# RWKV scan of a two-block layer stack on one core: step 11's mask before the update, squares and clamp behind the last context tap, blend in two instructions, centering and V's third tap one place later

## The chip, the cores and the metric

The kernel runs on one core of one Trainium2 chip. The metric is the time of one execution in device microseconds (us), given as the median of several runs. A second number, the span, is what one profiled execution took from its first to its last instruction. TensorE (PE) multiplies, VectorE (DVE), ScalarE (ACT) and GpSimd (POOL) do the elementwise work, SyncE (SP) issues the DMAs.

## The reference

A first block is an RWKV-7 mixer with a context, a spatial gating branch and an expert-choice feed-forward network; a second block has differential attention, a recurrent unit and neighbourhood attention. The change touches the RWKV part (`token_mixer`, `context_scan_states`) and one wait of the stage behind it. All is fp32. What matters, cut down:

```python
z = centred_shift(h @ w_in, taps)     # z[t] = y[t-1]*w0 + y[t]*w1 + y[t+1]*w2: three taps
r, k, v, dwf, dwb, daf, dab, dg = split(z)
d = exp(-exp(-softplus(-(w0 + tanh(dw) @ w2)) - 0.5))       # one for each direction
a = sigmoid(a0 + da @ a2)
kk = k * k_k;  kk = kk * rsqrt(maximum(sum(kk*kk), 1e-12))  # square, squares, clamp, root, invert
k_dir = k * (1 + (a - 1) * k_a)                             # blend: 1 + (a-1)*k_a, then times k
# scan forward and backward, over 256 context tokens and then 512 tokens:
S = S*d - (S kk)(kk*a)^T + v k^T ;  y = S r
y = ((y - mean) * rsqrt(var + eps)) * lnx_g + lnx_b         # center, variance, normed
y = (y + (sum(r*k*r_k)) * v) * (sigmoid(dg) @ g2)           # bonus, gated
```

The stage behind it (`stage_merge`) makes the gating branch and the outputs, and beside that the modulation vectors (`silu(c) @ ada_w`), in 20 column blocks of 512, on VectorE.

## The kernel before, in words

`stage_scan` treats the 16 heads in 8 pairs, 128 channels each. One pair is one turn j of the loops (turns 0 to 8; the ninth only finishes the last pair). The tokens, context and main, make 12 steps of 64; both directions are computed together. In place of a token-by-token scan, the system of a step is inverted in five levels, four steps at a time (a group).

Each turn has three stretches s (groups of four steps of this pair), each with five levels l, and each level two halves: places (s, l, 0) and (s, l, 1). Every engine walks through the same loops and has a function `beside(j, at)` that puts other work at each place: for the next pair (b = j + 1) projections, taps, decay, rates and the parts of kk and k; for the previous pair (a = j - 1) centering, variance, bonus and gate. So the order of the queues is written out by hand; only semaphores tie the engines together. In turn j the scan's own steps 8 to 11 of pair j - 1 run in stretch 0, steps 0 to 7 of pair j in stretches 1 and 2.

What TensorE does at a level: the product X times the part (L752), with tokens turned in between (`product_beside_tokens`, L737) and keys (L909); right side and scores (L854, L721); `beside` of the first half; solve (L894); correct (L832, L834); read-out (L921); `beside` of the second half. At level 4 there is no solve; there `correct_last` (L814, L817) waits for two things: the level's mask from VectorE, and `xt0_done`, GpSimd's word that the next group's start matrix is ready. The chain to that is: `parts` on VectorE (L1626, masks the scores of a step), `part_moved` on ScalarE (L1265, copies four steps), `xt0` on GpSimd (L1466 and L1468, two passes over 128x512).

VectorE at a level: `mask` (L1539), `beside`, `update` (L1550, L1552), `state` (L1565, L1569), `beside`. ScalarE: `negate` (L1207), `beside`, `solved` (L1212, which TensorE's read-out waits for), `beside`. GpSimd's queue in a turn: `xt0(j, 1)`, `reverse_v(j + 1, 0)` (L1509, waits for V's context taps), `xt0(j, 2)`, `new_k(j + 1)` (L1476 to L1478, wait for blend), `scaled_k`, `xt0(j + 1, 0)`, and so on.

Short results of TensorE go through `Scratch`: three banks of PSUM, handed out in turn in the order in which TensorE's program takes them. Whoever takes one waits until the last user of that bank has moved its contents:

```python
def take(self, pe, *what):
    n, R = len(self.nth), len(self.banks)      # R = 3
    self.nth[what] = n
    if n >= R:
        pe.wait_ge(self.moved[n % R], n // R)
```

Names at the places of the change: `squares` (L684) sums k's squares per head on TensorE from `square` (L1276); `clamp` (L1639), `root` (L1281), `invert` (L1644), `widen` (L1286), then transposes back to TensorE (L695) and `unit_k` (L1651). `shift` applies taps (L1607, L1609, L1611: first, second, third). `blend` is L1294, `gated` L1719. `center` (L950) writes the centered y, which ScalarE copies twice (L1328, L1329). TensorE's projection of the next pair's K (L673, at (0, 0, 1)) waits until all taps of V are done. SyncE's queue (weights of the next pair) isn't changed.

In `stage_merge` TensorE makes a list of outputs; ahead of output 32 (the first "mix") stand value, u and gate outputs, then come mix 0, mix 1, a 0, mix 2, a 1. `conds_turned` says behind which output a column block of the modulation is summed over channels (L198). VectorE adds the bias (L206) once all 20 are turned, and only then empties the mix outputs' banks (L2171, L2172).

Of the kernel before, what the change touches and what calls it, by code (L numbers as in the profile page):

```python
# [502 lines left out]
def stage_scan(k, hT, w_low, low_loaded, th, da, sg, ya, spare, m, first_chunk, first_loaded, loose, h_scale):  # L503
# [20 lines left out]
    with ExitStack() as s:  # L524
# [91 lines left out]
        def _(pe):  # L616
# [28 lines left out]
            def context_of(j, d):  # L645

                if live(j):
                    from_low_rank(j, (("rate", d, 1), ("decay", 1 - d, 1)))
# [297 lines left out]
            def center(j):  # L946
                if live(j):
                    pe.wait_ge(S["y_copied"], j + 1)
                    o = sc.take(pe, "center", j)
                    sc.fill(mm(o[:], m["center"][:], yj[:], start=True, stop=True), "center", j)  # L950
# [29 lines left out]
            def beside(j, at):  # L980

                a, b = j - 1, j + 1
                if at == (0, 0, 0):
                    turn_params(b)
                if at == (0, 0, 1):
                    project(b, K_X, 0)
                if at == (0, 1, 0):
                    project(b, K_X, 1)
                    bonus(j)
                if at == (0, 1, 1):  # L990
                    project(b, K_X, 2)
                if at == (0, 2, 1):
                    project(b, K_X, 3)
                if at == (0, 2, 0):
                    both_directions(b, "rate")
                if at == (0, 3, 0):
                    both_directions(b, "decay")
                if at == (0, 3, 1):
                    to_tokens(j, "B", 0)
                if at == (0, 4, 0):  # L1000
                    context_of(b, 0)
                    to_tokens(j, "K", 0)
                if at == (0, 4, 1):
                    context_of(b, 1)
                    center(a)
                    project(b, K_V, 0)
                if at == (1, 0, 0):
                    variance(a)
                if at == (1, 0, 1):
                    project(b, K_V, 1)  # L1010
                if at == (1, 1, 0):
                    project(b, K_V, 2)
                    spread_rstd(a)
                if at == (1, 1, 1):
                    project(b, K_V, 3)
                if at == (1, 2, 1):
                    gate(a)
                if at == (1, 3, 1):
                    project(b, R_X, 0, KT)
                    project(b, R_X, 1, KT)  # L1020
                    squares(b)
                if at == (1, 4, 0):
                    project(b, R_X, 2, KT)
                if at == (1, 4, 1):
                    project(b, R_X, 3, KT)
                if at == (2, 0, 0):
                    spread_inverse(b)
                if at == (2, 0, 1):
                    project(b, R_X, 4, KT)
                if at == (2, 1, 0):  # L1030
                    project(b, R_X, 5, KT)
                if at == (2, 1, 1):
                    project(b, R_X, 6, KT)
                if at == (2, 2, 0):
                    project(b, R_X, 7, KT)
                if at == (2, 2, 1):
                    scores(b, 0)
                    scores(b, 2)
                if at == (2, 3, 1):
                    for i in range(3):  # L1040
                        project(b, V_X, i, KT)
                if at == (2, 4, 0):
                    for i in range(3, 5):
                        project(b, V_X, i, KT)
                if at == (2, 4, 1):
                    for i in range(5, KT):
                        project(b, V_X, i, KT)
# [152 lines left out]
        def _(act):  # L1200
            f = act.activation
# [84 lines left out]
                    f(sqj.rearrange("p (n c) -> p n c", c=HEAD), length[:].rearrange("p t h -> p (t h)").unsqueeze(2).to_broadcast([P, 2 * NT, HEAD]),  # L1286
                      ACT.Copy).then_inc(S["inverse_wide"], 1)

            def blend(j):

                if live(j):
                    for i in range(4):
                        sc.settled(act, "rate", j, i)
                    f(kt[:], ra[:], ACT.Identity, scale=col(j, 10), bias=col(j, 18)).then_inc(S["t1_done"], 1)  # L1294

            of_seg = (slice(0, CTX_STEPS), slice(CTX_STEPS, STEPS))
            each_way = lambda view: view.rearrange("p d (n t) -> p d n t", t=HEAD)
# [42 lines left out]
            def beside(j, at):  # L1340
                a, b = j - 1, j + 1
                if at == (0, 0, 0):
                    tokens(j, "V", 0)
                if at == (0, 2, 1):
                    rate(b, 0)
                    rate(b, 1)
                if at == (0, 3, 0):
                    decay(b, 0)
                if at == (0, 3, 1):
                    part_moved(j, 1)  # L1350
                    decay(b, 1)
                    tokens(j, "B", 0)
                if at == (0, 4, 0):
                    rate(b, 2)
                    decay(b, 3)
                    tokens(j, "K", 0)
                    copy_y(a)
                if at == (0, 4, 1):
                    x0(j, 1)
                    rate(b, 3)  # L1360
                    decay(b, 2)
                    centered(a)
                if at == (1, 0, 0):
                    tokens(j, "V", 1)
                    deviation(a)
                if at == (1, 0, 1):
                    widen_rstd(a)
                if at == (1, 1, 0):
                    tokens(j, "B", 1)
                if at == (1, 2, 0):  # L1370
                    tokens(j, "K", 1)
                if at == (1, 3, 0):
                    tokens(j, "V", 2)
                if at == (1, 3, 1):
                    square(b)
                    part_moved(j, 2)
                    root(b)
                if at == (1, 4, 0):
                    tokens(j, "B", 2)
                if at == (1, 4, 1):  # L1380
                    x0(j, 2)
                    widen(b)
                    if j == KT - 1:
                        act.wait_ge(S["ahead_mm"], 1)
                        sc.settled(act, "inverse", KT - 1, 0)
                        sc.settled(act, "inverse", KT - 1, 1)
                        t, o = AHEAD[0]
                        f(spare[:, t, 0:512], bank[o][:], ACT.Copy).then_inc(S["ahead_moved"], 1)
                if at == (2, 0, 0):
                    tokens(j, "K", 2)  # L1390
                    blend(b)
                if at == (2, 0, 1):
                    grow(b, 0)
                    shrink(b, 0)
                if at == (2, 1, 0):
                    grow(b, 1)
                if at == (2, 1, 1):
                    shrink(b, 1)
                if at == (2, 2, 0):
                    shrink_r(b)  # L1400
                if at == (2, 2, 1):
                    decay_over_step(b)
                if at == (2, 3, 1):
                    part_moved(b, 0)
                if at == (2, 4, 1):
                    x0(b, 0)
# [7 lines left out]
            def prologue():  # L1414
# [15 lines left out]
                decay_over_step(0)  # L1430
                for i in range(4):
                    rate(0, i)
                blend(0)
                part_moved(0, 0)
                x0(0, 0)
                act.wait_ge(S["low_shift"], low_no(LOW_GATE))
# [94 lines left out]
        def _(dve):  # L1531
# [188 lines left out]

            def beside(j, at):
                a, b = j - 1, j + 1
                if at[0] < 2 and at[1] < 4 and at[2] == (1 if at[0:2] == (1, 3) else 0):
                    parts(j, 4 + 4 * at[0] + at[1])
                if at == (0, 0, 0):
                    params(b)
                if at == (0, 1, 1):
                    bonus(j)
# [13 lines left out]
                    shift(b, K_V, (0,))  # L1742
                if at == (1, 2, 1):
                    shift(b, K_V, (1,))
                if at == (1, 3, 0):
                    shift(b, K_V, (2,))
                    gated(a)
                if at == (1, 3, 1):
                    clamp(b)
                if at == (1, 4, 0):  # L1750
                    invert(b)
                if at == (1, 4, 1):
                    running_sums(b, 1)
                if at == (2, 0, 1):
                    unit_k(b)
# [14 lines left out]
                    scaled_b(b, 1)  # L1770
                    scaled_q(b, 1)
                if at == (2, 4, 1):
                    shift(b, V_X)

            def low_shift(f):

# [51 lines left out]
def stage_merge(k, hT, ya, x1, retired, first_chunk, first_loaded, ring1, u, ys, gates, xn, aff, ring, w_in_ex, loose, lt, iota_i, iota):  # L1828
# [14 lines left out]
    for i in range(8):  # L1843
# [17 lines left out]
    CONDS_LOADED_BEHIND = {1: range(0, 2), 2: range(2, 4), 3: range(4, 6), 4: range(6, 9), 5: range(9, 12),  # L1861
                           6: range(12, 15), 7: range(15, 18), 8: range(18, len(ADA))}
    CONDS_TURNED_BY = {1: range(0, 3), 2: range(3, 6), 3: range(6, 9), 4: range(9, 12), 5: range(12, 14), 6: range(14, 17),
                       7: range(17, len(ADA))}
    conds_turned = {4 * c + 1 + len(AHEAD): CONDS_TURNED_BY[c] for c in CONDS_TURNED_BY}
    names = """x_in sgu_in ln1_in w_turned w_moved made moved_act moved_dve v_normed stats std iota_made iota_done lt_made row_mm row_moved
        diag_made l_stats l_std r_stats r_std sc2_made rows_mm rows_moved router_in normed turned turn_moved logits shifted e_done""".split()
    S = {n: k.sem("mg_" + n) for n in names}
# [1828 lines left out]
```

## Time and profile before

| what | us |
|---|---|
| median of 3 runs | 2960.75 (2954.12 to 2962.56) |
| the profiled execution, its own time | 2963.89 |
| its span | 2962.3 |
| PE busy | 2726.9 (92%) |
| DVE busy | 1170.3 (40%) |
| ACT busy | 608.7 (21%) |
| POOL busy | 265.6 (9%) |
| mean granted TensorE clock | 0.979 |

Busy times are sums over all instructions of an engine. The scan lies between some 100 and 880 us of the span; turn 3, from which most rows below are, begins at 402 and ends at 499, turn 7 begins at 793. In the profile's rows a line such as L1626 is the line of the kernel, and `arena`, `x` and `bank` are names of shared buffers. A matmul of fp32 is two records. Consecutive rows of one engine overlap a little, since instructions are pipelined.

### The profile page before, as it was taken

The numbers are of one execution on the slowest core, as the hardware profiler recorded it, in microseconds if no ns is written. First come the engines' busy times: TensorE is split into PE (matmuls) and PEld (weight loads), VectorE is DVE, ScalarE is ACT, GpSimd is POOL, SyncE is SP. The second block draws the span as 40 slices with busy tenths as digits, with TensorE's granted clock in tenths as the row PEclk, the third lists the DMA queues.
The fourth block names the chain that finished last, engine by engine and source line by source line (L and its number), as shares of the span: only waits on it lengthen the run. The fifth ranks groups of instructions, "written<-read, shape, count | busy, mean of one in ns | idle before, by whom it ended". The sixth has DMA issues, their size and how long they took to land. (4 is left out here: it accounts for less than half of the span.)

```text
span 2962.3 us, 69542 instructions
## 1 busy us (share of the span) xinstructions
PE 2726.9 (92%) x31106; PEld 1478.0 (50%) x31106; DVE 1170.3 (40%) x2615; ACT 608.7 (21%) x1254; POOL 265.6 (9%) x282
## 2 busy tenths in 40 slices
PE   6999999999989999979988988989886999999998
PEld 3667676777664445444343333433333555455553
DVE  4566556656634762271211221212013255423333
ACT  2324333333221100010000000000002344323322
POOL 1221122212200000010000000000000111110000
PEclk9999999999999999989999999999998999999999
DMA  5000000000007872349999999999994421042210
GB/s 206 27 25 21 21 20 26 21 21 18 33 5 267 301 256 85 133 195 377 431 430 431 430 430 431 431 430 430 431 430 170 144 59 37 0 134 64 63 34 29
DMA packets 188812, 557.41 MB, mean 188 GB/s; under 512 B 29452, under 2 KB 117026, under 8 KB 163958
## 3 DMA queue, kind: packets, MB, share of 16 engines
q1 hardware_dynamic: 188534, 553.19, 47.6%
q8 instruction: 237, 3.88, 0.5%
q14 instruction: 41, 0.34, 0.0%
HBM read 550.65 MB, written 2.24 MB: 187 GB/s over the span
## 5 line engine op out<-in xcount | busy, mean ns | idle before, releaser
L2338 PE MATMUL bank<-arena,xe 128*64 128x512 f32 x1024 | 351.9, 614 | 36.1 <-DMA gates<-in_exp_w_dram 19.9
L2338 PEld LDWEIGHTS bank<-arena,xe 128*64 128x64 f32 x1024 | 108.6, 141 | 189.5 <-issue 177.4
L673 PE MATMUL bank<-arena 128*128 128x512 f32 x384 | 191.9, 620 | 1.2 <-issue 1.2
L3361 PE MATMUL bank<-arena 128*128 128x512 f32 x384 | 173.8, 600 | 1.9 <-PEq L2656 1.9
L2338 PE MATMUL bank<-arena,hidT 128*64 128x512 f32 x512 | 170.0, 595 | 2.5 <-DMA gates<-in_exp_w_dram 2.0
L2789 PE MATMUL bank<-arena 128*128 128x512 f32 x320 | 145.2, 602 | 1.2 <-ACT arena L2937 1.2
L2551 DVE TENSOR_TENSOR x<-x,bank 128x512 f32<-128x512 f32 x64 | 43.7, 686 | 232.9 <-PE bank L2376 232.9
L2338 PE MATMUL bank<-mg_ring,xe 128*64 128x512 f32 x256 | 114.5, 601 | 20.0 <-DMA u<-in_exp_w_dram 20.0
L2338 PE MATMUL bank<-ys,xe 128*64 128x512 f32 x256 | 115.9, 606 | 16.5 <-DMA arena<-in_exp_w_dram 15.8
L2544 DVE TENSOR_TENSOR hid<-hid,bank 128x512 f32<-128x512 f32 x32 | 19.8, 682 | 280.3 <-PE bank L2338 280.3
L1539 DVE TENSOR_TENSOR pm<-bank,m_level 128x512 f32<-128x512 f32 x120 | 82.8, 690 | 102.3 <-PE bank L752 101.6
L2338 PE MATMUL bank<-gates,xe 128*64 128x512 f32 x256 | 118.2, 616 | 0.0
L2338 PE MATMUL bank<-u,xe 128*64 128x512 f32 x256 | 114.9, 602 | 0.0
L834 PE MATMUL bank<-XT,pm 64*64 64x32 f32 x3072 | 111.2, 220 | 2.2 <-issue 1.9
L832 PE MATMUL bank<-pm,XT 64*64 64x32 f32 x3072 | 107.0, 218 | 3.9 <-issue 2.2
L3361 PEld LDWEIGHTS bank<-arena 128*128 128x128 f32 x384 | 69.9, 190 | 81.1 <-issue 81.1
L752 PEld LDWEIGHTS bank<-X,px 64*64 64x64 f32 x2560 | 85.7, 135 | 44.6 <-issue 19.1
L832 PEld LDWEIGHTS bank<-pm,XT 64*64 64x64 f32 x3072 | 99.4, 135 | 6.7 <-issue 3.2
L752 PE MATMUL bank<-X,px 64*64 64x64 f32 x2560 | 98.4, 224 | 3.0 <-issue 1.5
L834 PEld LDWEIGHTS bank<-XT,pm 64*64 64x64 f32 x3072 | 99.4, 134 | 3.4 <-issue 3.3
L2789 PEld LDWEIGHTS bank<-arena 128*128 128x128 f32 x320 | 59.7, 193 | 74.0 <-issue 73.4
L1207 ACT ACTIVATE x<-bank 128x128 f32<-128x128 f32 x96 | 26.7, 278 | 331.7 <-PE bank L854 331.7
(523 smaller groups left out, 5542.1 us busy)
## 6 DMA issues: line engine op xcount, KB each, us to landing
arena<-in_exp_w_dram SPq DMA_DIRECT2D x96, 2048.0 KB, 26.7
gates<-in_exp_w_dram SPq DMA_DIRECT2D x24, 2048.0 KB, 29.9
ys<-in_exp_w_dram SPq DMA_DIRECT2D x24, 2048.0 KB, 26.7
mg_ring<-in_exp_w_dram SPq DMA_DIRECT2D x24, 2048.0 KB, 26.8
u<-in_exp_w_dram SPq DMA_DIRECT2D x24, 2048.0 KB, 31.3
ws_w<-in_ada_w_dram SPq DMA_DIRECT2D x40, 1024.0 KB, 5.6
arena<-in_odd_w_in_dram SPq DMA_DIRECT2D x32, 512.0 KB, 3.9
arena<-in_w_in_dram SPq DMA_DIRECT2D x24, 512.0 KB, 3.9
```

The lines of the kernel that those rows point to most:

```text
L673: last = mm(to[:], wj[:, c, i, :], hT[:, c, 0:T], start=(c == 0), stop=(c == KT - 1))
L752: last = mm(INV[c, cs(q)], part(4 * g + q // 2, q % 2, 0, 0)[h], X[h, (j * GROUPS + g) % 2, q, :], start=True, stop=True)
L832: mm(into(INV, h, q), XT[c, g, q, :], blocks(pm[c, q, :], b, 0), start=True, stop=True)
L834: last = mm(into(INVT, c, q), pm[c, q, :], blocks(XT[c, g, q, :], b, 1), start=True, stop=True)
L1207: f(rn, RIGHT.rearrange("p (d v) -> p d v", d=2), ACT.Copy, scale=-1.0).then_inc(S["r_neg"], 1)
L1539: tt(pm[:], INV[:].rearrange("p (q t) -> p q t", q=8), m["level"][:, l, :].unsqueeze(1).to_broadcast([P, 8, HEAD]), ALU.mult).then_inc(S[" ...
L2338: r[e] = mm(out[a, :], lhs[j][:, a], w[:, j, 512 * c:512 * c + 512], start=(first and j == 0), stop=(last and j == len(lhs) - 1), skip_gro ...
L2544: dve.tensor_tensor(hid[:, f, :], hid[:, f, :], bank[4 + f][:], ALU.mult).then_inc(S["hid_made"], 1)
L2551: dve.tensor_tensor(x1[:, n, c], x1[:, n, c], bank[scatter_bank(q, o)][:], ALU.add).then_inc(S["added"], 1)
L2789: last = mm(o[:], w[:, c, i, :], hT[:, i, :], start=(i == 0), stop=(i == KT - 1))
L3361: last = mm(o[:], w[:, i, t, :], hT[:, t, :], start=(t == 0), stop=(t == KT - 1))
```

## The change

At (1, 3) VectorE's `parts` of step 11 runs in the first half, behind the mask and ahead of the update, and the third tap of K's and V's context and `gated` go to the second half. ScalarE copies the part before it squares. `squares` on TensorE, `clamp` on VectorE and `root` on ScalarE go from (1, 3, 1) to (1, 4, 0), `invert` from (1, 4, 0) to (1, 4, 1). `blend` becomes two instructions, one per direction, at (2, 0, 0) and (2, 0, 1). `center` stands behind the first projection piece of K's and V's context at (0, 4, 1). V's third tap goes from the end of a turn, (2, 4, 1), to (0, 0, 0) of the next, behind `parts`. In `stage_merge` column block 19 is turned behind output 34 instead of 32.

```diff
@@ TensorE, beside
                 if at == (0, 4, 1):
                     context_of(b, 1)
+                    project(b, K_V, 0)
                     center(a)
-                    project(b, K_V, 0)
@@
                 if at == (1, 3, 1):
                     project(b, R_X, 0, KT)
                     project(b, R_X, 1, KT)
+                if at == (1, 4, 0):
                     squares(b)
-                if at == (1, 4, 0):
                     project(b, R_X, 2, KT)
@@ ScalarE
-            def blend(j):
+            def blend(j, way):
 
                 if live(j):
-                    for i in range(4):
-                        sc.settled(act, "rate", j, i)
-                    f(kt[:], ra[:], ACT.Identity, scale=col(j, 10), bias=col(j, 18)).then_inc(S["t1_done"], 1)
+                    if way == 0:
+                        for i in range(4):
+                            sc.settled(act, "rate", j, i)
+                    last = f(kt[:, way], ra[:, way], ACT.Identity, scale=col(j, 10), bias=col(j, 18))
+                    if way == 1:
+                        last.then_inc(S["t1_done"], 1)
@@
                 if at == (1, 3, 1):
+                    part_moved(j, 2)
                     square(b)
-                    part_moved(j, 2)
-                    root(b)
                 if at == (1, 4, 0):
                     tokens(j, "B", 2)
+                    root(b)
@@
                 if at == (2, 0, 0):
                     tokens(j, "K", 2)
-                    blend(b)
+                    blend(b, 0)
                 if at == (2, 0, 1):
+                    blend(b, 1)
                     grow(b, 0)
                     shrink(b, 0)
@@ VectorE, beside
-                if at[0] < 2 and at[1] < 4 and at[2] == (1 if at[0:2] == (1, 3) else 0):
+                if at[0] < 2 and at[1] < 4 and at[2] == 0:
                     parts(j, 4 + 4 * at[0] + at[1])
                 if at == (0, 0, 0):
+                    if j:
+                        shift(j, V_X, (2,))
                     params(b)
@@
-                if at == (1, 3, 0):
+                if at == (1, 3, 1):
                     shift(b, K_V, (2,))
                     gated(a)
-                if at == (1, 3, 1):
+                if at == (1, 4, 0):
                     clamp(b)
-                if at == (1, 4, 0):
+                if at == (1, 4, 1):
                     invert(b)
-                if at == (1, 4, 1):
                     running_sums(b, 1)
@@
                 if at == (2, 4, 1):
-                    shift(b, V_X)
+                    shift(b, V_X, (0, 1))
@@ stage_merge
-                       7: range(17, len(ADA))}
+                       7: range(17, 19)}
     conds_turned = {4 * c + 1 + len(AHEAD): CONDS_TURNED_BY[c] for c in CONDS_TURNED_BY}
+    conds_turned[34] = range(19, len(ADA))
```

## Rows read from the trace of the kernel before

**Rows 1.** The page, part 1: busy us of each engine (share of the span).

```profile
PE 2726.9 (92%) x31106; PEld 1478.0 (50%) x31106; DVE 1170.3 (40%) x2615; ACT 608.7 (21%) x1254; POOL 265.6 (9%) x282
```

**Rows 2.** Waits of PE, 165 to 860 us: engine line <- released by: total us, times, longest.

```profile
PE bank L814 <- issue: 15.0, 12, 3.0
...
PE bank L921 <- ACT x L1212: 3.5, 8, 0.5
...
PE bank L950 <- ACT X L1271: 2.1, 6, 0.4
```

**Rows 3.** Timeline of DVE, turn 3, (1, 3): start, us, engine, line [idle before <- releaser].

```profile
454.03 0.69 DVE L1539 TENSOR_TENSOR pm<-bank,m_level 128x512 f32<-128x512 f32 x1 [0.22 <-PE bank L752]
454.64 0.47 DVE L1611 SCALAR_TENSOR_TENSOR kj<-bank,pcol,kj 128x255 f32<-128x255 f32 x1
...
455.54 0.75 DVE L1719 SCALAR_TENSOR_TENSOR arena<-arena,pcol,bank 128x512 f32<-128x512 f32 x1
...
457.99 0.29 DVE L1569 TENSOR_TENSOR ZG<-Z,g 128x128 f32<-128x128 f32 x1
458.20 0.68 DVE L1626 TENSOR_TENSOR px<-bank,m_part 128x512 f32<-128x512 f32 x1
```

**Rows 4.** Timeline of ACT, turn 3, (1, 3) to (1, 4).

```profile
459.07 1.27 ACT L1265 ACTIVATE XT<-px 64x512 f32<-64x512 f32 x2 [2.41 <-DVE px L1626]
...
464.84 0.83 ACT L1286 ACTIVATE x<-k_length 128x768 f32<-128x768 f32 x1
```

**Rows 5.** Timeline of POOL, turn 3, (1, 3) to (1, 4).

```profile
455.57 0.40 POOL L1509 COPY vjr<-vj 128x256 f32<-128x256 f32 x1 [27.33 <-DVE vj L1611]
460.42 1.27 POOL L1466 TENSOR_TENSOR XT<-XT,m_pair 128x512 f32<-128x512 f32 x1 [4.45 <-ACT XT L1265]
461.77 1.26 POOL L1468 TENSOR_TENSOR XT<-XT,m_id 128x512 f32<-128x512 f32 x1
```

**Rows 6.** Timeline of PE, turn 3, (1, 3) to (1, 4).

```profile
458.86 0.58 PE L684 MATMUL bank<-head_ones,x 128*32 128x2 f32 x48
459.37 0.27 PE L752 MATMUL bank<-X,px 64*64 64x64 f32 x2
...
460.47 1.12 PE L673 MATMUL bank<-arena 128*128 128x512 f32 x2
463.13 0.25 PE L814 MATMUL bank<-XT,pm 64*64 64x32 f32 x2 [1.54 <-issue]
```

**Rows 7.** Timeline of PE, turn 7: L814 of (1, 4), read-out of (2, 0).

```profile
849.84 0.32 PE L814 MATMUL bank<-XT,pm 64*64 64x32 f32 x2 [2.98 <-issue]
...
857.89 0.42 PE L921 MATMUL bank<-x 64*64 64x64 f32 x7
```

**Rows 8.** Windows: stretch, length, busy us (instructions) of the engines, PEclk, DMA, GB/s.

```profile
849.84:856.08 6.24, 5.54 (x153) 5.01 (x154) 1.11 (x2) 1.69 (x4) 0.00 (x0) 0.50 0.03 5
...
463.13:470.13 7.00, 6.19 (x232) 4.88 (x232) 3.21 (x5) 3.85 (x7) 0.14 (x1) 1.00 0.02 5
...
1115.50:1118.90 3.40, 3.40 (x8) 1.73 (x7) 3.33 (x11) 0.00 (x0) 0.00 (x0) 0.50 0.77 293
```

**Rows 9.** Timeline of ACT, turn 3, (2, 0).

```profile
468.25 1.67 ACT L1294 ACTIVATE kt<-ra,pcol 128x1536 f32<-128x1536 f32 x1
469.81 0.27 ACT L1212 ACTIVATE x<-bank 128x128 f32<-128x128 f32 x1
```

**Rows 10.** Timeline of PE, turn 3, (2, 0).

```profile
470.13 0.45 PE L921 MATMUL bank<-x 64*64 64x64 f32 x8 [0.49 <-ACT x L1212]
```

**Rows 11.** Timeline of DVE, turn 3, (2, 0).

```profile
471.14 0.81 DVE L1569 TENSOR_TENSOR ZG<-Z,g 128x128 f32<-128x128 f32 x1
```

**Rows 12.** Timeline of DVE, end of turn 3.

```profile
498.32 0.75 DVE L1611 SCALAR_TENSOR_TENSOR vj<-bank,pcol,vj 128x511 f32<-128x511 f32 x1
```

**Rows 13.** Timeline of PE in the merge stage.

```profile
1114.35 0.43 PE L198 MATMUL bank<-ones,arena 128*32 128x1 f32 x32 [1.92 <-DVE arena L186]
```

**Rows 14.** Timeline of DVE in the merge stage.

```profile
1117.46 0.69 DVE L2172 TENSOR_TENSOR ys<-ys,u 128x512 f32<-128x512 f32 x1
```

More of the change, by code:

```diff
@@ L1432, in prologue @@
                     rate(0, i)
-                blend(0)
+                blend(0, 0)
+                blend(0, 1)
                 part_moved(0, 0)
```

## The prediction

> **What bounds the kernel now.** I read the page's busy shares first, then the waits of TensorE over seven turns of the scan, then the timelines of single places. TensorE is busy 92% of the span [rows 1], so a moved step counts only where TensorE now waits for it. Its list of waits [rows 2] gives three places that the change touches: L814, the correction at place (1,4), 15.0 us in 12 waits; L921, the read-out at (2,0), 3.5 us in 8, released by ScalarE; and L950, the centering at (0,4), 2.1 us in 6, released by a ScalarE copy. The list names "issue" for L814 and so hides the cause; the timelines show it.
>
> In turn 3 VectorE ends ZG (L1569) at 458.28 and the mask of step 11 (L1626) runs only then, from 458.20 [rows 3]; ScalarE copies the part from 459.07 for 1.27 us [rows 4]; GpSimd makes two passes, 460.42 to 463.03 [rows 5]; TensorE, whose two projection matmuls began at 460.47 and took 1.12, starts L814 at 463.13, 0.1 us behind GpSimd, after 1.54 us of idleness [rows 6]. That is a chain mask, copy, two passes, correction, and it starts too late.
>
> **Part 1, step 11's mask and its company.** The mask now follows the level's mask, which ends at 454.72 [rows 3]. It comes 3 us earlier, and the whole chain with it. The stall doesn't vanish by its 1.5 us, because two things move the other way.
>
> First, `squares` moves behind the product of (1,4), so the turned tokens B of group 2 are now taken one place before it, and take over the scratch bank that `squares` had: the one held by `gate` of the turn before. TensorE must wait there for `gated`, and `gated` has moved behind update and state. Queued ahead of it on VectorE are both context taps (454.64 to 455.54, 0.90 us as a pair) and then itself (0.75). It starts where L1626 did: 458.20 + 0.90 + 0.75 = 459.85, and 0.1 us for the release: 459.95. TensorE could have begun the product at 458.86, where `squares` began [rows 6]. So 1.1 us of new waiting, with the whole product, key update, right side and correction queued behind it.
> Then the sum for turn 3: 459.95, product 1.10 (459.37 to 460.47), squares 0.51 (458.86 to 459.37), projection 1.07 = 462.63, against 463.13: 0.5 us gained.
>
> Second, GpSimd reverses V's context between the two passes of group 1 and of group 2, and it waits for the last context tap. That tap now ends at 459.07; 0.06 release, 0.40 reversal, 0.04, 2.61 for the passes, 0.1: L814 not before 462.3 [rows 3, 5]. That is hidden under 462.63 by 0.3 us and is what is late next if the bank's wait were shorter. Square, clamp, root and invert move with the tap: `square` runs 459.1 to 460.1, before TensorE wants it at 461.1; the level's mask waits for the product and ends at 461.9; clamp and root end before the correction does at 463.6, and `invert` (0.22 us) stands ahead of a scan (1.8 us) with 0.8 us free behind it. Cost nothing; without that cover `widen` (0.83 [rows 4]) would slip by the 0.2 of `invert`.
>
> The same sum over each turn's own times gives 0.8 in turn 0 (no gate there, GpSimd decides), 0 in turn 1 (the copy is earlier there), 0.2 in turn 2, 0.5 in turns 3 to 6, and in turn 7 (no tap, no squares) L814 from 849.84 to 847.9, 1.9 us. Sum 4.9. Bounds: 0, if a new wait eats it all, and 13.6, the idleness at these eight places (15.0 less what stands elsewhere).
>
> **The clock in turn 7.** There TensorE idles 2.98 us before L814 [rows 7], and the granted clock is 0.50, the lower level of 1.2 GHz, in the 6.24 us behind it [rows 8]. From L814 to the read-out of (2,0) the turn takes 8.05 us [rows 7]; turn 3 takes 7.00 (463.13 to 470.13), some 1.1 of it the blend's stall and the inverse's transposes, which turn 7 lacks. So the low level costs 2.2 us. The new wait there is 1.1 us, shorter than the 1.54 of turn 3 [rows 6], behind which the clock stayed at 1.00 [rows 8]. I take 2.2; the ends are 0 and 3.1, half of 6.24.
>
> **Part 2, blend in halves.** ScalarE spends 1.67 us on blend and copies U (L1212) only at 469.81 [rows 9]; the read-out starts at 470.13 after 0.49 us [rows 10]. A half costs about 0.86: the 768-element row takes 0.83 [rows 4]. U is then copied at 469.0, and the read-out follows the correction at 469.5: 0.6 us in turns 2 to 6, 0.2 in turn 0, none in turn 1, where TensorE is later anyway; sum 3.2. The second half then precedes the table load, which starts at 470.1 as before; the next negation is wanted at 472.6, and ScalarE is free at 472.6. GpSimd starts on K 0.1 us later and is needed at 479. Ends: 0 and 3.9, 0.65 in six turns.
> ZG (L1569) took 0.81 us here, not its 0.29, beside GpSimd's pass over K [rows 11, 3]. It will be asked for 0.6 us sooner but ends when that pass does, at 471.95; unit_k and the next level's mask then end at 473.7, and TensorE wants that mask at 473.7. So no loss, but no room either; if it slips, up to 0.1 us a turn is given back.
> The Trainium skill, SBUF — State Buffer, "Who interferes with whom", says that VectorE and GpSimd share a port pair that one instruction holds to its end, also for a VectorE operation with two SBUF inputs. ZG is such an operation and the trace agrees (0.81 against 0.29). By this rule it blocks for what is left of GpSimd's pass, as reckoned; if it did not, ZG would be early and the sum would be the same.
>
> **Part 3, centering behind the projection.** L950 waits for the copy of X (L1271), which frees its bank, 0.35 us on average [rows 2]; matmuls back to back overlap by 0.07, so 0.43 is filled by the projection's 2.0 us. Six turns: 2.6. The centered copies on ScalarE come 1.5 us later, still 0.3 before the next negation. Ends 0 and 2.8.
>
> **Part 4, V's third tap.** 0.75 us on VectorE go from ahead of the first mask of a turn (498.32 to 499.07) to behind parts(4) [rows 12]. The mask ended 0.1 after TensorE wanted it; 7 times 0.1 = 0.7. The tap now ends at 500.7; TensorE's projection of K waits for it at 501.1, and the parameter copies behind it end as the correction does. Ends: -1.5 (0.2 a turn) and 0.7. The prologue pays 0.1 for a second blend instruction.
>
> **Part 5, the last modulation column block.** Now TensorE waits 1.92 us for VectorE [rows 13] after the first mix output, and the granted clock is 0.50 for 3.4 us behind that [rows 8], which costs up to 1.7. Moved behind that output, the wait is gone, but VectorE empties the mix banks only after this block: 3.4 us from it (1114.78 to 1118.15 [rows 13, 14]), and TensorE has only the 0.9 of one mix output for it before it needs the first bank again. New wait 2.5, so 0.6 lost, and 1.7 won only if the clock stays up. The nearest row says it won't: a shorter wait stood ahead of that low stretch. I take -0.6; ends -0.6 and +1.1.
>
> **Sum.** 4.9 + 2.2 + 3.2 + 2.6 + 0.7 - 0.1 - 0.6 = 12.9. The profiled execution took 2963.9 (its span 2962.3 and 1.6 around it), so 2951.0 of its kind. The median of the runs is 3.1 lower, 2960.75: 2947.9, 2948 in round numbers. A change of 0.3%, 8.9 us, is what can be told from none: the bounds are 2951.9 and 2969.6.
>
> **Rivals.**
> A. Part of it is given back: the low level stays in turn 7 (2.2) and the blend's gain is lost to the mask behind the blocked ZG or to the next negation, both without room (3.2). 12.9 - 5.4 = 7.5: 2953.3. For it: both margins are 0.0 to 0.1. Against: turn 3 shows the order fit.
> B. The wait for `gated` is not there, and GpSimd decides: 0.35 more in turns 3 to 6, 0.9 more in turns 1 and 2 together, 1.1 in turn 7, 3.4 in all: 2944.5. For it: only if another bank is taken. Against: three banks in turn, counted.
> C. Slower. The new 1.1 us wait lies before every (1,4) beside other small ones; if the clock falls behind it in turns 1 to 6 as in turn 7, each fall costs 2.2 (turn 7) to 3.4: 13.2 to 20.5, against 12.9 less turn 7's 2.2. That is 2.5 to 9.8 above before: 2963 to 2970.5, say 2967. It decides from a wait of more than 1.54 us on, which these turns had without a fall; mine are 1.1.
> The Trainium skill, TensorE: Matmul & The Clock Gate, "A second HAM failure mode: psum-queue depth-cycling", says that frequent short idle spells between matmul groups can make the clock go up and down. That would be rival C; in turns 3 to 6 of this trace no row shows it.
>
> **Chances.** Forecast 0.50 (own range 2944 to 2952), A 0.28, B 0.10, C 0.12. Faster by over 0.3%: 0.47 + 0.03 of A + B's 0.10 = 0.60. Within: 0.03 + 0.25 + 0.05 = 0.33. Slower: 0.07. The range reaches from below B to above A, 2941 to 2959; it leaves out C and B's far end.
>
> **What would show it.** L1626 of step 11 at about 0.96 us behind the mask's start; L814's idleness gone, a new TensorE wait of about 1.1 ahead of the product of (1,4) (L752), released by L1719; each of turns 3 to 6 shorter by 1.6 us; L921 with no wait for L1212; L950 with none; turn 7 without a fall to 0.50; the wait at L198 gone, and one of 2.5 before an L2014. It is wrong if L814 still waits over 0.3 us for GpSimd, or if turns don't get shorter.

## The result, and the profile after

| what | before | after |
|---|---|---|
| median of the runs beside each other, us | 2961.19 (2954.12 to 2963.65, 6 runs) | 2972.09 (2969.93 to 2976.26, 6 runs) |
| span of the profiled execution, us | 2962.3 | 2970.6 |
| mean granted TensorE clock | 0.979 | 0.975 |

The ratio is 1.0042 [1.0029, 1.0055]: 0.4% slower, where 0.4% faster was forecast. The engines do the same work (part 1 of the page after, against [rows 1]):

```profile
PE 2735.7 (92%) x31106; PEld 1480.7 (50%) x31106; DVE 1172.7 (39%) x2615; ACT 611.3 (21%) x1262; POOL 264.8 (9%) x282
```

TensorE is busy 8.8 us longer with the same 31106 matmuls, about all of the 8.3 between the spans. Its idle time is the same in sum: waits went and others came. These are its waits, 165 to 860 us (columns as in [rows 2]):

```profile
PE bank L673 <- DVE vj L1616: 15.6, 7, 2.3
...
PE bank L814 <- issue: 2.0, 4, 1.2
PE bank L752 <- DVE arena L1724: 1.7, 1, 1.7
...
PE bank L921 <- ACT x L1212: 1.0, 3, 0.3
```

L814 fell from 15.0 to 2.0, L921 from 3.5 to 1.0, and L950 is gone, as foretold. But a line that before didn't have leads the list: the projection of the next pair (L673) waits 2.2 to 2.3 us for `vj`, the third context tap (L1616 now), once in each of turns 0 to 6. The place in turn 3, first VectorE, then TensorE of the kernel after:

```profile
457.71 0.69 DVE L1544 TENSOR_TENSOR pm<-bank,m_level 128x512 f32<-128x512 f32 x1 [0.22 <-PE bank L752]
458.60 0.69 DVE L1631 TENSOR_TENSOR px<-bank,m_part 128x512 f32<-128x512 f32 x1 [0.20 <-PE bank L721]
460.40 0.42 DVE L1555 TENSOR_TENSOR X<-X,bank 128x256 f32<-128x256 f32 x1 [1.11 <-PE bank L834]
...
461.57 0.29 DVE L1574 TENSOR_TENSOR ZG<-Z,g 128x128 f32<-128x128 f32 x1
461.78 0.48 DVE L1616 SCALAR_TENSOR_TENSOR kj<-bank,pcol,kj 128x255 f32<-128x255 f32 x1
462.18 0.47 DVE L1616 SCALAR_TENSOR_TENSOR vj<-bank,pcol,vj 128x255 f32<-128x255 f32 x1
462.68 0.75 DVE L1724 SCALAR_TENSOR_TENSOR arena<-arena,pcol,bank 128x512 f32<-128x512 f32 x1
```

```profile
460.17 0.43 PE L921 MATMUL bank<-x 64*64 64x64 f32 x8
462.80 2.04 PE L673 MATMUL bank<-arena 128*128 128x512 f32 x2 [2.19 <-DVE vj L1616]
```

In the kernel before the same projection followed the read-out at once (TensorE of before, turn 3):

```profile
456.59 0.43 PE L921 MATMUL bank<-x 64*64 64x64 f32 x8
456.95 1.99 PE L673 MATMUL bank<-arena 128*128 128x512 f32 x4
```

The reader sees why. Both kernels project R at (1, 3, 1) into the PSUM bank that held K's and V's context, and the code says so: `project` waits for `shift_no(j, which - 1)`, the last tap of the projection before it. In before that tap had ended at 455.51, ahead of the update; now it stands behind update and state and ends at 462.65. And the two matmul records took 2.04 us, where before's four took 1.99: the granted clock fell. The windows of after at the low level in turn 3, in turn 7 and in the merge stage (columns as in [rows 8]):

```profile
461.90:468.70 6.80, 5.91 (x92) 3.28 (x96) 1.70 (x4) 1.08 (x2) 2.89 (x3) 0.50 0.32 89
854.40:857.80 3.40, 3.40 (x66) 2.00 (x61) 0.69 (x1) 0.60 (x1) 0.23 (x1) 0.51 0.07 19
1127.50:1134.30 6.80, 5.92 (x7) 2.52 (x8) 3.98 (x7) 0.00 (x0) 0.00 (x0) 0.50 0.00 0
```

Such a stretch begins in the wait at L673 or just behind it in turns 0 to 4 and 6, for 3.4 or 6.8 us each; before had none there. From the level's mask of (1, 3) to that of (1, 4), turns 0 to 6 are longer by 4.1, 3.1, 3.1, 4.3, 4.3, 1.8 and 3.1 us; the least is turn 5, the one without a low stretch. With turn 7 that is 26.2 us, and (1, 4) gives 13.3 back. The whole scan, from its first to its last such mask, went from 762.2 to 768.5. Of the 8.3 us between the spans 6.3 are then in the scan; the stretch between the scan and the first mix gains 2 (a low stretch of before at 880 is gone), the one from there to the last a loses 2.1 (Part 5); 2 us are behind it, where nothing was changed: over the twelve traces of this case that last part takes between 1722 and 1728 us, so 2 us there in one execution say nothing of an edit.

### The profile page after: what moved, and what is told of

Its sections match the earlier page's. It is cut to its first block and busy times, and to the rows that moved or that the text cites. A ratio compares the mean times of both kernels' runs of the same rounds, so it can differ in the third digit from the quotient of the medians.

```text
span 2970.6 us, 69557 instructions
## 1 busy us (share of the span) xinstructions
PE 2735.7 (92%) x31106; PEld 1480.7 (50%) x31106; DVE 1172.7 (39%) x2615; ACT 611.3 (21%) x1262; POOL 264.8 (9%) x282
## 5 line engine op out<-in xcount | busy, mean ns | idle before, releaser
L673 PE MATMUL bank<-arena 128*128 128x512 f32 x384 | 200.5, 644 | 16.7 <-DVE vj L1616 15.6
L3368 PE MATMUL bank<-arena 128*128 128x512 f32 x384 | 176.6, 608 | 1.9 <-PEq L2663 1.9
L2796 PE MATMUL bank<-arena 128*128 128x512 f32 x320 | 144.5, 600 | 1.2 <-ACT arena L2944 1.2
L752 PEld LDWEIGHTS bank<-X,px 64*64 64x64 f32 x2560 | 88.3, 140 | 56.3 <-issue 28.7
L834 PE MATMUL bank<-XT,pm 64*64 64x32 f32 x3072 | 111.4, 220 | 3.6 <-issue 3.5
L3368 PEld LDWEIGHTS bank<-arena 128*128 128x128 f32 x384 | 71.0, 193 | 82.8 <-issue 82.8
L752 PE MATMUL bank<-X,px 64*64 64x64 f32 x2560 | 100.1, 229 | 3.3 <-DVE arena L1724 1.7
L673 PEld LDWEIGHTS bank<-arena 128*128 128x128 f32 x384 | 66.8, 195 | 70.8 <-issue 65.5
L834 PEld LDWEIGHTS bank<-XT,pm 64*64 64x64 f32 x3072 | 99.6, 134 | 4.7 <-issue 4.5
L2796 PEld LDWEIGHTS bank<-arena 128*128 128x128 f32 x320 | 59.5, 192 | 73.6 <-issue 73.1
## 6 DMA issues: line engine op xcount, KB each, us to landing
ys<-in_exp_w_dram SPq DMA_DIRECT2D x24, 2048.0 KB, 26.2
```

The costliest lines, as they stand in the source:

```text
L673: last = mm(to[:], wj[:, c, i, :], hT[:, c, 0:T], start=(c == 0), stop=(c == KT - 1))
L752: last = mm(INV[c, cs(q)], part(4 * g + q // 2, q % 2, 0, 0)[h], X[h, (j * GROUPS + g) % 2, q, :], start=True, stop=True)
L834: last = mm(into(INVT, c, q), pm[c, q, :], blocks(XT[c, g, q, :], b, 1), start=True, stop=True)
L2796: last = mm(o[:], w[:, c, i, :], hT[:, i, :], start=(i == 0), stop=(i == KT - 1))
L3368: last = mm(o[:], w[:, i, t, :], hT[:, t, :], start=(t == 0), stop=(t == KT - 1))
```

## Experiments

Each ran beside the kernel before on its chip (medians of before 2962.4 to 2963.6). "Early" is the first half of (1, 3), ahead of the update, "late" the second half, behind update and state.

**1. The tap early again** (the change, but the tap ahead of step 11's mask).

```diff
+                if at == (1, 3, 0):
+                    shift(b, K_V, (2,))
                 if at[0] < 2 and at[1] < 4 and at[2] == 0:
                     parts(j, 4 + 4 * at[0] + at[1])
@@
                 if at == (1, 3, 1):
-                    shift(b, K_V, (2,))
                     gated(a)
```

> The changed kernel, but the third tap of K's and V's context is back in the first half of (1,3), ahead of step 11's mask; gated stays in the second half. Theory 1: R's projection at (1,3,1) waits for that tap, because R and K/V share one bank, and TensorE's clock falls behind the wait. Then L673 has no wait there, no low stretch of the clock follows in turns 1 to 6, the time from the mask of (1,3) to that of (2,0) is some 2 us shorter a turn than in the changed kernel, a wait of about 1.1 us for gated (L1724's line) stands before the product of (1,4), and the time is about 2957 us. Theory 2: the loss comes from the scratch banks' new order, that is from waiting for gated or for squares: the time stays near 2970.

Measured 2958.88 (11 runs), ratio 0.9991 [0.9980, 1.0002]. The wait at L673 is gone, and the time is 13.2 us lower. By the traces 9.2 of that lie in the scan, and 2.9 in the merge stage, where the low stretch at 1127.5 didn't come this time. What TensorE waits for now, and VectorE and GpSimd in turn 3:

```profile
PE bank L752 <- DVE arena L1724: 6.8, 7, 1.7
PE bank L684 <- issue: 6.6, 3, 2.5
```

```profile
461.19 1.41 DVE L1574 TENSOR_TENSOR ZG<-Z,g 128x128 f32<-128x128 f32 x1
462.52 0.73 DVE L1724 SCALAR_TENSOR_TENSOR arena<-arena,pcol,bank 128x512 f32<-128x512 f32 x1
```

```profile
461.18 1.27 POOL L1471 TENSOR_TENSOR XT<-XT,m_pair 128x512 f32<-128x512 f32 x1 [1.80 <-ACT XT L1265]
462.53 1.27 POOL L1473 TENSOR_TENSOR XT<-XT,m_id 128x512 f32<-128x512 f32 x1
```

The wait for `gated` (L752 for `arena`) is the one that the prediction reckoned, 1.1 us; here it is 1.26 in turn 3. With GpSimd's chain early, its first pass falls on ZG, which took 1.41 us instead of 0.29 and pushed `gated`. And there is a wait that nobody expected, up to 2.5 us at L684 in turns 1 to 3, released by nothing in the profile (TensorE, turn 3), with the DMA view of 459 to 470 us:

```profile
464.49 0.55 PE L684 MATMUL bank<-head_ones,x 128*32 128x2 f32 x44
466.94 0.27 PE L684 MATMUL bank<-head_ones,x 128*32 128x2 f32 x4 [1.89 <-issue]
```

```profile
GB/s 0 0 0 0 0 0 0 0 0 0 0 0 0 0 0 0 0 0 0 166 110 41 78 138 177 264 335 350 326 168 32 20 0 60 0 0 0 0 0 0
...
q1 hardware_dynamic: 1184, 0.59, 19.2%
q8 instruction: 2, 0.03, 1.5%
```

It sits in the middle of one line's matmuls, all 48 of them ready. By the packets' times a block of instructions landed at 465.66, in the 512 KB weight load (464.3 to 467.8), and TensorE went on 1.3 us later. In before the load's data came at 457.3 to 460.8; SyncE's queue issues it behind a wait for `gated`, so it came later with it. That the fetch causes the stall is an inference from times.

So Theory 1's time came (2957), but not its account: in turns 1 to 3 a low stretch of 3.4 to 6.8 us begins in or just behind the stop at L684, and there (1, 3) and (1, 4) together are 1.3, 2.8 and 0.9 us longer than in the change; over all eight turns they are 6.8 shorter. That the sum hit is in part luck.

**2. Tap, mask of step 11 and `gated` all early**, in this order.

```diff
+                if at == (1, 3, 0):
+                    shift(b, K_V, (2,))
                 if at[0] < 2 and at[1] < 4 and at[2] == 0:
                     parts(j, 4 + 4 * at[0] + at[1])
@@
-                if at == (1, 3, 1):
-                    shift(b, K_V, (2,))
+                if at == (1, 3, 0):
                     gated(a)
```

> As e1_tap_back, and gated too is back in the first half of (1,3), behind step 11's mask. Theory 1 with the bank's wait of the prediction: no wait before the product of (1,4) either, L814 has no wait, each turn 1.1 us shorter than e1_tap_back: about 2950 us. If the three scratch banks do not tie the product of (1,4) to gated, it takes the same time as e1_tap_back.

Measured 2941.91 (5 runs), ratio 0.9926 [0.9913, 0.9940]: better than either theory. In turn 3 the projection follows the read-out at once, and the clock stays up (TensorE, and a window):

```profile
453.62 0.43 PE L921 MATMUL bank<-x 64*64 64x64 f32 x8
453.98 1.98 PE L673 MATMUL bank<-arena 128*128 128x512 f32 x4
...
459.32 0.25 PE L814 MATMUL bank<-XT,pm 64*64 64x32 f32 x2
```

```profile
452.50:459.30 6.80, 6.10 (x189) 3.83 (x180) 4.48 (x9) 3.28 (x6) 2.95 (x3) 1.00 0.33 89
```

No wait for the tap or for `gated` is left, and L814 has 1.2 us in 4; (1, 3) and (1, 4) are 16.9 us shorter than before over the eight turns. Forecast for the prediction's own order were 4.9 plus 2.2: its sum was held down by the wait for `gated` and, right behind it, by GpSimd, which waits for the late tap.

**3. Part 1 alone**: the kernel before with the steps of (1, 3) and (1, 4) moved, nothing else (the lines of the change for those places, on TensorE, ScalarE and VectorE).

> The kernel before with part 1 alone (step 11's mask, context tap and gated, squares, clamp, root and invert, ScalarE's order at (1,3)); blend, centering, V's tap and the merge stage as before. Theory 1: it carries more than the whole loss, 12.9 us by the places (1,3) and (1,4) of the two traces: about 2974 us. Rival: the loss is spread over the other parts too, V's third tap (0.59 us a turn at (0,0)) above all, and this kernel stays under 2968.

Measured 2972.64 (10 runs), ratio 1.0037 [1.0021, 1.0053], the time of the whole change. The same line heads its list of waits:

```profile
PE bank L673 <- DVE vj L1611: 15.6, 7, 2.3
```

So Part 1 alone carries the loss; what the other parts add can't be seen in the runs.

**4. Filling the wait.** The change, with five 128x128 matmuls on the layer's input (`hT`) put ahead of the projection, in the time in which TensorE waits. They write to a bank that the next product overwrites.

```diff
                 if at == (1, 3, 1):
+                    if live(b):
+                        pe.wait_ge(S["x_done"], level_no(j, 1, 3))
+                        for c in range(5):
+                            mm(INV[:, 0:P], hT[:, c, 0:P], hT[:, c, 0:P], start=True, stop=True, skip_group_check=True)
                     project(b, R_X, 0, KT)
```

> The changed kernel with five extra 128x128 matmuls ahead of R's projection at (1,3,1), written to a bank that is overwritten by the next product, so that TensorE works while it would wait for the tap. Output unchanged. Theory 1a: the wait costs 2.4 us a turn and the fall of the clock behind it 1.3 (3.4 us stretches) to 2.5 (6.8 us stretches), some 11 us over six turns; with the wait filled no fall follows and the time is about 2961. Theory 1b: the falls have another cause; the time stays at 2972 or above.

Measured 2976.73 (5 runs), ratio 1.0044 [1.0030, 1.0058]: not faster, as Theory 1b had it. Yet at its place it did what Theory 1a said: TensorE's wait at L673 fell to 1.2 us (with 4.3 in 7 ahead of the added matmuls, which wait for VectorE's update), the low stretches behind it went in turns 1 to 6, and (1, 3) with (1, 4) came out 10.7 us shorter than in the change (11 expected). At (0, 0) the same 10.7 us were lost again, and 5.4 more at (0, 4), much of it in stops of one line:

```profile
PE bank L834 <- issue: 14.4, 15, 2.9
```

These are stalls like that of experiment 1, now 1.0 to 2.9 us at one place of each of turns 1 to 7. The added instructions shift which matmuls the block boundaries fall on; that this moved the stops is inferred. The theory is borne out by the place, not by the total.

**5. The small parts alone**: before with the blend in halves, the centering and V's tap.

> The kernel before with parts 2, 3 and 4 only: blend in halves, centering behind the projection, V's third tap one place later. By the places of the changed kernel's trace: blend -3.5 us, centering -2.3, V's tap +0.5, in all -5.3: some 2957, ratio 0.998. Rival: these parts too lose time by themselves, V's tap above all, and the kernel is not faster than before.

Measured 2963.89 (12 runs), ratio 1.0004 [0.9993, 1.0014]: nothing, as the rival had it. L950 is gone from its waits and L921 fell to 1.0, so each edit did its work. But V's tap costs 6.1 us at (0, 0), where (2, 4) gains 5.0, and stops without a releaser of over 0.75 us, L814 aside, come to 9.1 us in 8 in the scan, against 5.0 in 5 in before.

**6. The merge stage's edit alone.**

> The kernel before with part 5 only: column block 19 turned behind output 34. The changed kernel's trace has a wait of 2.6 us before the output a 1 and a 6.8 us stretch of the clock's lower level behind it, 2.1 us more than before from mix 0 to the start of a 2. Theory: +2 us here too, ratio 1.0005 to 1.001. Rival: this was one execution's clock, and the part gains 1 us or more.

Measured 2962.39 (12 runs), ratio 0.9995 [0.9983, 1.0007]: the interval just reaches the 2 us, so the runs don't show them and don't rule them out. In the trace the first mix to the last a take 0.8 us more than in before. The wait of the forecast is there (TensorE, behind it the granted clock is 0.50 for 3.4 us):

```profile
1122.88 8.83 PE L2015 MATMUL bank<-arena 128*128 128x512 f32 x16 [2.34 <-DVE ys L2173]
```

**7. Version 2 with block 19 behind output 33.**

```diff
-    conds_turned[34] = range(19, len(ADA))
+    conds_turned[33] = range(19, len(ADA))
```

> e2_gate_early, with column block 19 turned behind output 33 (mix 1) in place of 34. The wait for VectorE's sum is 1.92 less mix 1's 0.9, about 1.0 us, and VectorE has the seven microseconds of output a 0 to empty the banks, so no wait before a 1 and no fall of the clock: 4 us less than e2_gate_early, some 2938. Rival: the banks of mix 0 and mix 1 still hold TensorE up, and the time stays as in e2_gate_early.

Measured 2940.26 (6 runs), ratio 0.9931 [0.9911, 0.9951]. One wait of 1.38 us remains (1.0 forecast), without a low stretch behind it; first mix to last a is 1.2 us shorter than in version 2, where 4 were forecast. By the runs it can't be told from it.

**8. Version 2 with V's third tap back at the end of the turn.**

> e2_gate_early with V's third tap back at the end of a turn. Theory: that move is neutral (mask 0.6 to 0.8 us earlier, the next level as much later), so the time stays within 1.5 us of e2_gate_early. Rival: the 2.5 us that turns 1 and 2 lose at (0,0) with a fall of the clock come from this tap; then this kernel is 4 us faster than e2_gate_early.

Measured 2940.84 (6 runs), ratio 0.9920 [0.9902, 0.9937], the same as version 2 within the runs. In the trace (0, 0) is 8.6 us shorter and (2, 4) 6.6 longer; 4.8 of the 8.6 are in turns 1 and 2, whose low stretches are gone.

**9. Both, 7 and 8.**

> The version with tap and gate early, V's third tap back at the end of the turn, and the last modulation column block behind output 33. Theory: the two last edits gave 1.1 us (tap and gate early to block at 33: 2941.9 to 2940.3) and 1.1 us (to V's tap back: 2940.8) singly and lie in different stages, so they add: 2939.5, ratio 0.992. Rival: the clock's falls and the instruction fetches come out another way in each arrangement, and the sum is 2 to 4 us off that in either direction.

Measured 2938.16 (2934.45 to 2941.64, 6 runs), ratio 0.9913 [0.9898, 0.9929]: the lowest median, 1.3 below the forecast. The runs tell it from neither 7 nor 8, so that the two gains add is not shown.

**10. The tap alone late**: version 2, with only the tap at (1, 3, 1).

```diff
-                if at == (1, 3, 0):
-                    shift(b, K_V, (2,))
                 if at[0] < 2 and at[1] < 4 and at[2] == 0:
                     parts(j, 4 + 4 * at[0] + at[1])
@@
+                if at == (1, 3, 1):
+                    shift(b, K_V, (2,))
                 if at == (1, 4, 0):
                     clamp(b)
```

> As the version with tap and gate early, but K's and V's third context tap alone stands behind update and state at (1,3,1); gated stays ahead. It completes the square of the two orders (both late 2972.1, gated late alone 2958.9, both early 2941.9). Theory: the projection at L673 waits for the tap, 2.3 us in each of turns 0 to 6, the clock falls behind it in most turns, and gated's wait at L752 is gone; the tap is then worth about what it was with gated late, 13 us: 2955. Rival 1: the projection's wait is all that counts and gated's hides under it: 2970. Rival 2: without gated's wait the tap's wait falls where TensorE has queued nothing else late and costs 16 us (7 times 2.3) plus six falls of 1.3 to 2.5: up to 2970 as well, but with the places (1,4) and (2,0) as quick as in the early version; under rival 1 they are slower.

Measured 2969.46 (2957.50 to 2974.62, 12 runs), ratio 1.0017 [1.0003, 1.0030]; its median stands 27.6 us above version 2. The runs spread widely, seven between 2969 and 2975 and five between 2957 and 2964; the profiled one, 2971.54, is of the upper group. All twelve lie over 13 us above the slowest of version 2. The theory of 13 us falls, and both rivals' totals come near; of their marks it is rival 2's that are there, (1, 4) and (2, 0) as quick as in version 2 (together 13.4 us under before against 11.7). The mark is a weak one, since in the change they are 12.1 under before. This closes the square:

| | tap early | tap late |
|---|---|---|
| `gated` early | 2941.9 | 2969.5 |
| `gated` late | 2958.9 | 2972.1 (the change) |

By the ratios, row by row, it is 0.9926, 1.0017, 0.9991 and 1.0042, the same picture: with the tap early a late `gated` costs 17 to 19 us, with the tap late 3 to 7. The two losses don't add: TensorE stands at L673 until the tap is done, and while it stands there `gated` gets done as well. The wait in the list and in turn 3, and the window behind it:

```profile
PE bank L673 <- DVE vj L1616: 15.1, 7, 2.3
```

```profile
462.79 0.34 PE L921 MATMUL bank<-x 64*64 64x64 f32 x6
465.33 1.19 PE L673 MATMUL bank<-arena 128*128 128x512 f32 x1 [2.19 <-DVE vj L1616]
```

```profile
464.50:471.30 6.80, 5.97 (x96) 3.35 (x100) 0.88 (x3) 1.14 (x2) 2.88 (x3) 0.50 0.23 69
```

It also gives the price of a fall by itself. Against version 2, the interval from (1, 3) to (1, 4) is longer by 2.1 and 2.4 us in turns 1 and 5, which have the wait and no low stretch behind it; by 4.2 in turn 0, with one of 3.4 us; by 5.0 to 5.2 in turns 2, 3, 4 and 6, with one of 6.8. So a wait of 2.2 costs about that much, a fall behind it some 2 or 2.8 more. Over turns 0 to 6 that is 29.0, of which the waits are 15.1.

## Why the forecast was wrong, step by step

**Part 1 failed, in the sentence "TensorE could have begun the product at 458.86".** It took for granted that the projection ahead of `squares` runs as before, at 456.95 in turn 3. Of the moved tap the prediction counted three waiters: GpSimd's reversal, ScalarE's `square` and, through `gated` behind it, TensorE's product. The fourth, the projection of R at (1, 3, 1), it did not list, although it knew the pattern: Part 4 names the same wait for V's taps and K's projection. In the trace of before this wait is invisible, since the tap was done 1.4 us ahead of it. The missed wait is 2.2 us in each of seven turns, 15.6 in all, and the clock falls behind most of them. Taking the tap back gives 13.2 us with `gated` late and 27.6 with it early (experiments 1 and 10).

**The wait for `gated` was sized right and judged wrong.** In the change it is left in turn 7 alone, since in the others TensorE stands at L673 meanwhile. With the stand at L673 gone (experiment 1) it is there, 1.26 in turn 3 (1.1 was said) and 6.8 in seven turns. But it was priced as a delay alone. Beside it the weight load came later, TensorE stood 6.6 us at L684 without a releaser, and low stretches followed; taken away (experiments 1 to 2) it is worth 17.0 us, 15.0 of them in the scan, where rival B gave 3.4.

**The clock: rival C's mechanism, with another wait.** The prediction gave C little, since its new waits of 1.1 us were under the 1.54 that these turns had without a fall. The waits that came were 2.2, and in six of seven turns the clock fell in or behind them. But 1.1 was no safe value either: in before TensorE stood 1.22 us ahead of L909 in turn 7, until 797.89, and from 798.1 the clock is at its lower level (before, a wait and a window):

```profile
PE bank L909 <- issue: 1.2, 1, 1.2
```

```profile
798.00:801.40 3.40, 3.40 (x46) 2.28 (x46) 1.38 (x2) 0.28 (x1) 0.00 (x0) 0.51 0.03 10
```

C's price, 2.2 to 3.4 a fall, is close to the measured 2 to 2.8; its total, 2963 to 2970.5, was built on the wrong wait and ends 1.6 below the result. In turn 7 the fall at L814 went, but the wait for `gated`, 1.74 us there, has a 3.4 us one behind it, and of 4.1 forecast for the turn's two places (1.9 and 2.2) 1.4 came. The Trainium skill, TensorE: Matmul & The Clock Gate, "A second HAM failure mode: psum-queue depth-cycling", speaks of frequent short idle spells between matmul groups that make the clock go up and down. The traces agree in part: here the clock falls in or behind single waits of 1.2 to 2.3 us. Turns 1 and 5 of experiment 10 and the wait of 2.34 us in version 2's merge stage have no fall behind them, so such a wait doesn't always do it.

**Step 11's chain** went as reckoned: its mask starts 0.89 behind the level's (0.96 was said), and L814 waits 2.0 us in all, not 15.0. What was said to be late next, GpSimd's passes behind the tap, is there too (they end at 465.67), hidden behind the projection and the product.

**Part 2** (3.2): places (2, 0) and (2, 1) are 3.5 us shorter. But 0.6 of it is in turn 7, which has no blend, and without Part 1 (experiment 5) turns 0 to 6 give 2.3. So the step was right and the term somewhat high: a half took 1.03, not 0.86, and (2, 0) grows by 0.3 to 0.4 us in five turns, while (2, 1) shrinks by 0.7 in six. ZG is held by GpSimd's pass to its end, as said (1.50 us in turn 3). **Part 3** (2.6): (0, 4) and (1, 0) give 2.3; in experiment 5 (0, 4) gives 2.6 and (1, 0) takes 1.7 back. Near. **Part 4** (0.7): (2, 4) gains 4.2, and (0, 0) loses 4.7. The term said that the tap at (0, 0) is free because K's projection comes later; what it left out is the update of its own place. In before VectorE idled only 0.39 us ahead of that update, and the tap takes 0.75: the update has no idle time ahead of it now.

**Part 5** (-0.6): the wait of 2.5 is there, 2.34 of idleness, at the place named. What follows it differs from trace to trace: a low stretch of 6.8 us in the change, one of 3.4 in experiment 6, none in version 2. From the first mix to the last a that makes 2.1 more than in before, 0.8 more and 0.9 less, around the -0.6 of the term.

**What stays open**: what makes TensorE stand without a releaser (the last section has what the traces say), which took up much of what experiment 5 should have gained; what decides whether the clock falls behind a wait; and why experiment 10's runs lie in two groups.

## What to carry to other kernels

When a producer is moved later, list its waiters from the code, semaphore by semaphore, not from the profile's waits: a wait that was always met in time leaves no row, and it is the one that appears. Give a new wait of TensorE a range, not its length alone: here 2.2 us cost 2.1 to 2.4 where the clock stayed up and 4.2 to 5.2 where it fell. And of two steps moved behind the same update, test each by itself: their waits can hide one another, so that mending one shows half.

## What the runs showed of the hardware beyond that

TensorE stops for 0.8 to 3 us inside or between ready matmuls, with no semaphore that explains it, at places that shift when a few instructions are added (L834 in experiment 4: 14.4 us in 15 stops; L684 in experiment 1: 6.6 in 3). Between 165 and 860 us the change and experiments 1, 2 and 4 have 37 such stops of over 0.75 us. By the packets' times every one of them ends 1.2 to 1.6 us after a 16 KB block of instructions has landed, though a block lands only every 4 us or so; and the six longest, 1.9 to 2.9 us, all have the data of a load beside them. In experiment 1 the queue with these blocks (q8) brings 156 in that stretch, while TensorE starts some 40,000 of the 42,000 instructions counted, so nearly all must be TensorE's own. This speaks for its instruction supply as the cause; no run changes that supply alone, so it is not shown. Ratios of 0.1% between kernels that differ by a few TensorE instructions can then not be read as the edit's price alone.

ZG, a VectorE operation with two SBUF inputs, took 1.41 us beside a GpSimd pass that ran from 461.18 to 462.45, and 0.29 alone, more than the 0.81 of [rows 11]. The Trainium skill, SBUF — State Buffer, "Who interferes with whom", says that a VectorE instruction with two SBUF inputs contends with a GpSimd instruction that reads SBUF. The trace agrees: ZG ends 0.15 us behind that pass.
